# Weight sums of a Strassen product: DVE additions or accumulating transfers from DRAM

## The chip, the cores and the metric

One NeuronCore of one Trainium2 chip runs the whole kernel. The metric is device time in microseconds (us) of one execution, the median of 3 runs. One more execution was taken with the profiler, and all rows below come from that one.

## The reference, cut to what matters

The reference is one encoder block for 512 tokens of width 2048: an RMS norm, one input projection, two attention mixers with gates, the output projection, a residual and a last RMS norm. What matters here is its end:

```python
mixed = jnp.concatenate([out_a, out_b], axis=-1)      # 512 x 2048
x = x + jnp.einsum('bsc,cd->bsd', mixed, w_out)       # w_out 2048 x 2048
return rms_norm(x, final_norm_w)
```

All is float32. The kernel multiplies in a faster format: it splits each operand into a high part (rounded) and a low part (what is left), and a product of two operands takes three matmuls (high x high, low x high, high x low; function `three`, lines 1396 to 1402).

## The kernel before, in words

The kernel is written engine by engine, each with its own instruction stream and semaphores; the order of the work is written out by hand. The output projection comes last. Output columns 0 to 1023 are computed directly. Columns 1024 to 2047 (blocks 2 and 3 of 512 columns) are computed by Strassen's scheme of seven products M1 to M7, over two halves of the tokens, of the input and of the columns. It is done in 16 visits. In each visit one 1 MB piece of `w_out` is used: four slots of 128 x 512, in the buffer `t_raw[v % 4]`.

- Visits 0 to 7 compute M2, M3 and M4. Visits 8 to 15 compute M5, M1, M6 and M7. A late visit has 24 matmuls of 512 columns: 12 for M5 and M1 (slots 0 and 1, group 0), then 12 for M6 and M7 (slots 2 and 3, group 1). Visits 14 and 15 are interleaved (lines 1820 to 1839), with all of both visits' M1 and M5 of the first token quarter ahead of any M6.
- In a late visit the piece holds, in slots 0 to 3, the blocks B11, B22, B12 and B21 of the weights. M1 needs B11 + B22, M5 needs B22, M6 needs B11 + B12, and M7 needs B21 + B22.
- SyncE (SP) loads piece v (line 324) when PE is through with visit v - 4, because there are four buffers. `t_landed[v % 4]` tells of the landing.
- VectorE (DVE) makes the sums in `part_sums(v)` (lines 1248 to 1257): for v of 8 or more, line 1255 adds slots 0 and 1 to slots 2 and 3 (the sums of M6 and M7, 1024 elements a partition), and line 1257 adds slot 1 to slot 0 (the sum of M1, 512 elements).
- ScalarE (ACT) makes the high parts in `part_high(v, g)` (lines 715 to 732), group 0 and then group 1 of each visit, when the sum is there and the `t_hi` buffer of two visits before is free.
- DVE makes the low parts in `part_low(v, g)` (lines 1259 to 1264), in place. PE waits for `t_low[0]` before group 0 and for `t_low[1]` before group 1 (lines 1797 and 1808).
- The order of DVE (lines 1324 to 1344) is: low(v,0), sums(v+1), low(v,1) for v up to 8; then eight additions from PSUM into the rows `y` (lines 1330 to 1336, function `add`, line 1277), which free the banks into which visit 8 accumulates M1, M6 and M7 (`y_added`, lines 1804 to 1817); then low(9,0), low(9,1), sums(10); and then low(v,0), sums(v+1), low(v,1) again.
- GpSimd (POOL) has little to do at this stage: it multiplies finished blocks of `y` by the final gain (`gained`, lines 399 to 402, called at lines 411 to 421), and at the end it scales some of them (line 427).
- The tail behind the last visit is additions from PSUM on DVE, squares on ACT, the root, the scaling and the stores (lines 1365 to 1391, 802 to 815 and 325 to 330).

```python
            for v in range(2, 9):
                part_low(v, 0)
                part_sums(v + 1)
                part_low(v, 1)
...
            for v in range(10, VISITS):
                part_low(v, 0)
                if v < VISITS - 1:
                    part_sums(v + 1)
                part_low(v, 1)
```

Of the kernel before, what the change touches and what calls it, by code (L numbers as in the profile page):

```python
# [6 lines left out]
ALU = mybir.AluOpType  # L7
# [93 lines left out]
def build(nc, w_stream, w_pairs, x_t, x_nat, gains, final_w, tables, out):  # L101
    with ExitStack() as ctx:  # L102
        def sem(name):
            return ctx.enter_context(nc.semaphore(name))
# [8 lines left out]
        def at(name, shape, dt, offset):  # L113
            return nc.alloc_sbuf_tensor_at(name, shape, dt, offset=offset)
# [29 lines left out]
        t_raw = [at(f"t_raw{n}", [P, 4, PART], F32, o) for n, o in enumerate(t_at)]  # L144
# [82 lines left out]
        u_at = [(r_rstd, r_rstd + 3 * KB), (r_rstd + 6 * KB, r_rstd + 9 * KB), (r_kr, r_kr + 3 * KB)]  # L227
        u_at += [(r_mixed + 6 * KB * n, r_mixed + 6 * KB * n + 3 * KB) for n in range(4)] + [(r_mixed + 24 * KB, r_kr + 6 * KB)]
        u_hi = [at(f"u_hi{j}", [P, 3, 256], F32R, o) for j, (o, _) in enumerate(u_at)]
        u_lo = [at(f"u_lo{j}", [P, 3, 256], F32R, o) for j, (_, o) in enumerate(u_at)]  # L230
        fw = [at(f"fw{n}", [P, SEQ], F32, o) for n, o in enumerate((r_ckv + 6 * KB, r_mixed + 28 * KB, r_mixed + 30 * KB, r4 + 32 * KB))]

# [12 lines left out]
        def part_slots(v, g):  # L245
            return slice(2, 4) if g == 1 else slice(1, 2) if v < 8 else slice(0, 2)
# [17 lines left out]
        fold_landed, kr_folded = sem("fold_landed"), sem("kr_folded")  # L264
        y0_landed, y1_landed, y_landed, fw_landed, fws_landed = sem("y0_landed"), sem("y1_landed"), sem("y_landed"), sem("fw_landed"), sem("fws_landed")
        fw1_landed = sem("fw1_landed")
        t_landed = [sem(f"t_landed{n}") for n in range(4)]
        u_summed, u_high, u_low, p_summed, p_high, p_low = sem("u_summed"), sem("u_high"), sem("u_low"), sem("p_summed"), sem("p_high"), sem("p_low")
        t_summed, t_high, t_used, m_done, y_added = sem("t_summed"), sem("t_high"), sem("t_used"), sem("m_done"), sem("y_added")
        t_low = [sem("t_low0"), sem("t_low1")]  # L270
# [63 lines left out]
        def _(pool):  # L334
            def low_part(c, s):
                pool.wait_ge(w_hi_ready, c + 1)
                pool.tensor_tensor(w_lo[:, s % HL, :], w_raw[:, s % RAW, :], w_hi[:, s % HL, :].bitcast(F32), ALU.subtract)\  # L337
                    .then_inc(w_lo_ready, 1)
# [60 lines left out]
            def gained(t, n):  # L399

                cols = slice(SEQ * n, SEQ * n + SEQ)
                pool.tensor_tensor(y[:, t, cols], y[:, t, cols], fw[n][:, :], ALU.mult).then_inc(o_gained, 1)  # L402

            for c in range(WO0 + 4 + AHEAD, WO0 + 16):
                low_part(c, c)
                if c == WO0 + 12:
                    pool.wait_ge(fw_landed, 16)
                    for t in range(TOK):
                        pool.wait_ge(o_squared, t + 2)
                        gained(t, 0)  # L410
            pool.wait_ge(fw1_landed, 16)
            for t in range(TOK):
                pool.wait_ge(o_squared, 4 + t + 2)
                pool.wait_ge(t_low[1], 4 + t)
                gained(t, 1)
            pool.wait_ge(fws_landed, 32)
            for q in range(2):
                pool.wait_ge(o_squared, 8 + q + 2)
                gained(2 * q + 1, 2)
            pool.wait_ge(o_squared, 12)  # L420
            gained(0, 3)

# [13 lines left out]
        def _(act):  # L436
# [218 lines left out]
            for p in range(PAIRS):  # L655
                f = 0
# [58 lines left out]
            def part_high(v, g):  # L715

                if g == 0 and v < 8:
                    act.wait_ge(t_landed[v % 4], 16 * (v // 4) + 16)
                else:
                    act.wait_ge(t_summed, v + 1 if v < 8 else 2 * v - 6 - (g == 1))  # L720
                if v == 0:
                    act.wait_ge(w_used, WO0 + 14)
                elif v == 1:
                    act.wait_ge(o_done, 8)
                elif v < 9:
                    act.wait_ge(t_used, 2 * v - 3 + g)
                elif v == 9:
                    act.wait_ge(m_done, 6 if g else 2)
                else:
                    act.wait_ge(t_used, 2 * v - 5 + g)  # L730
                s = part_slots(v, g)
                act.activation(t_hi[v % 2][:, s, :], t_raw[v % 4][:, s, :], ACT.Copy).then_inc(t_high, 1)  # L732
# [24 lines left out]
            pair_high(4)  # L757
            unit_high(5)
            part_high(0, 0)
            pair_high(5)  # L760
            unit_high(6)
            part_high(0, 1)
            pair_high(6)
            unit_high(7)
            act.wait_ge(u_low, 8)
            residual_rows(0)
            part_high(1, 0)
            pair_high(7)
            part_high(1, 1)
# [49 lines left out]
        def _(dve):  # L819
# [348 lines left out]
            for p in range(PAIRS):  # L1168
                f, late, behind = 0, None, ()
# [78 lines left out]
            def part_sums(v):  # L1248

                raw = t_raw[v % 4]  # L1250
                dve.wait_ge(t_landed[v % 4], 16 * (v // 4) + 16)
                if v < 8:
                    dve.tensor_tensor(raw[:, 2:4, :], raw[:, 0:2, :], raw[:, 2:4, :], ALU.subtract).then_inc(t_summed, 1)
                else:
                    dve.tensor_tensor(raw[:, 2:4, :], raw[:, 2:4, :], raw[:, 0:2, :], ALU.add).then_inc(t_summed, 1)
                    dve.wait_ge(t_summed, 2 * v - 7)
                    dve.tensor_tensor(raw[:, 0, :], raw[:, 0, :], raw[:, 1, :], ALU.add).then_inc(t_summed, 1)  # L1257

            def part_low(v, g):
# [39 lines left out]
            pair_sums(3)  # L1299
            pair_low(3)  # L1300
            part_sums(0)
            pair_sums(4)
            unit_sums(5)
# [6 lines left out]
            unit_low(6)  # L1310
            part_low(0, 1)
            part_sums(1)
            pair_sums(6)
            unit_sums(7)
# [5 lines left out]
            part_low(1, 0)  # L1320
            pair_low(7)
            part_sums(2)
            part_low(1, 1)
            for v in range(2, 9):
# [601 lines left out]
```

## Time and profile before

| what | value |
|---|---|
| median of 3 runs | 672.02 us (671.67 to 672.49) |
| profiled execution, its own time | 671.85 us |
| span of its instructions | 670.1 us |
| PE matmul busy | 654.7 us (98%) |
| DVE busy | 442.2 us (66%) |
| ACT busy | 331.3 us (49%) |
| POOL busy | 280.1 us (42%) |
| HBM read, written | 77.22 MB, 4.19 MB |

The execution's own time is 1.75 us more than the span, which is what lies around the instructions. A matmul row is 0.39 us long but the next one starts 0.227 us after it, so the matmul rows overlap, and the pace is to be read from the starts. The granted clock of TensorE is 1.00 of full speed in the stretches of 10 us from 500 to 660 us.

### The profile page before, as it was taken

Reading aid. Unit: us, or ns where it says so; the run is one execution under the profiler, and the core shown is the slowest. Engines: PE = TensorE matmul, PEld = TensorE weight load, DVE = VectorE, ACT = ScalarE, POOL = GpSimd, SP = SyncE. Lnnn points to the kernel's source line nnn. Section 1 sums busy time; section 2 is a strip of 40 time slices with the busy share of each in tenths; the row PEclk is TensorE's granted clock in tenths of the full one; section 3 lists DMA queues with packets and bytes.
Section 4 is the critical chain, followed back from the end, with each engine's and each line's share of the span. In section 5 each row is a group of like instructions: output and inputs, shape, how many; then the busy total and the mean of one; then the engine's idle time right before and its main releaser. Section 6 shows DMA issues by size and latency. Waiting matters only on the chain. (4 is left out here: it accounts for less than half of the span.)

```text
span 670.1 us, 8800 instructions
## 1 busy us (share of the span) xinstructions
PE 654.7 (98%) x3126; PEld 548.4 (82%) x3126; DVE 442.2 (66%) x702; ACT 331.3 (49%) x623; POOL 280.1 (42%) x135
## 2 busy tenths in 40 slices
PE   9999999999999999999999999999999999999893
PEld 8888888888888888888888888888888888787782
DVE  6788132889684554654645667777553769899985
ACT  6743231311343753763664566877864533543534
POOL 0044443454244433433532526747868483020204
PEclk9999999999999999999999999999999999999997
DMA  8742322232232222222212413213124813576416
GB/s 293 256 141 96 103 94 95 83 105 95 94 94 96 75 83 95 92 65 95 95 64 94 126 35 124 64 64 96 32 72 177 299 65 113 233 259 236 180 64 251
DMA packets 21656, 81.96 MB, mean 122 GB/s; under 512 B 2416, under 2 KB 2672, under 8 KB 19568
## 3 DMA queue, kind: packets, MB, share of 16 engines
q1 hardware_dynamic: 18000, 73.41, 32.1%
q10 hardware_dynamic: 3616, 8.02, 3.4%
q8 instruction: 25, 0.41, 0.2%
q14 instruction: 15, 0.12, 0.1%
HBM read 77.22 MB, written 4.19 MB: 122 GB/s over the span
## 5 line engine op out<-in xcount | busy, mean ns | idle before, releaser
L337 POOL TENSOR_TENSOR w_lo<-w_raw,w_hi 128x1024 fp32r<-128x1024 f32 x84 | 206.0, 2458 | 269.7 <-ACT w_hi L442 269.6
L1398 PE MATMUL bank<-x_hi,w_hi 128*128 128x512 f32 x496 | 193.7, 390 | 0.0
L1401 PE MATMUL bank<-x_hi,w_lo 128*128 128x512 f32 x496 | 193.3, 390 | 0.0
L1402 PE MATMUL bank<-x_lo,w_hi 128*128 128x512 f32 x496 | 193.2, 390 | 0.0
L442 ACT ACTIVATE w_hi<-w_raw 128x1024 fp32r<-128x1024 f32 x93 | 98.1, 1055 | 130.0 <-PE bank L1398 109.1
L1402 PEld LDWEIGHTS bank<-x_lo,w_hi 128*128 128x128 f32 x496 | 93.1, 188 | 19.7
L1398 PEld LDWEIGHTS bank<-x_hi,w_hi 128*128 128x128 f32 x496 | 93.2, 188 | 18.8 <-DVE mixed L1078 0.5
L1401 PEld LDWEIGHTS bank<-x_hi,w_lo 128*128 128x128 f32 x496 | 93.2, 188 | 18.0
L402 POOL TENSOR_TENSOR y<-y,fw 128x512 f32<-128x512 f32 x11 | 17.6, 1616 | 80.1 <-ACT junk L705 44.4
L1398 PE MATMUL bank<-w_hi,mx_hi 128*128 128x512 f32 x128 | 50.3, 393 | 0.0
L1402 PE MATMUL bank<-w_lo,mx_hi 128*128 128x512 f32 x128 | 49.9, 390 | 0.0
L1401 PE MATMUL bank<-w_hi,mx_lo 128*128 128x512 f32 x128 | 49.9, 390 | 0.0
L732 ACT ACTIVATE t_hi<-t_raw 128x1024 fp32r<-128x1024 f32 (+1 forms) x32 | 29.8, 950 | 37.7 <-DVE t_raw L1257 19.5
L540 ACT ACTIVATE bank<-pa,st_a 128x128 f32<-128x128 f32 x64 | 22.8, 356 | 43.2 <-DVE st_a L992 43.2
L1264 DVE TENSOR_TENSOR t_lo<-t_raw,t_hi 128x1024 fp32r<-128x1024 f32 (+1 forms) x32 | 35.2, 1120 | 5.3 <-ACT t_hi L732 5.3
L1007 DVE TENSOR_TENSOR pta_lo<-bank,pta_hi 128x512 fp32r<-128x512 f32 x16 | 11.1, 692 | 32.1 <-ACT pta_hi L547 32.0
L1402 PEld LDWEIGHTS bank<-w_lo,mx_hi 128*128 128x128 f32 x128 | 24.0, 188 | 5.1
L1401 PEld LDWEIGHTS bank<-w_hi,mx_lo 128*128 128x128 f32 x128 | 24.1, 188 | 4.7
L895 DVE TENSOR_TENSOR t<-bank,sin_r 32x512 f32<-32x512 f32 x40 | 27.5, 687 | 0.5
L1398 PEld LDWEIGHTS bank<-w_hi,mx_hi 128*128 128x128 f32 x128 | 24.0, 188 | 4.6
L1015 DVE TENSOR_TENSOR mixed<-bank,o_low 64x256 f32<-64x256 f32 x32 | 13.5, 422 | 21.6 <-ACT o_low L554 21.4
L1398 PE MATMUL bank<-t_hi,mx_hi 128*128 128x512 f32 x64 | 25.3, 395 | 2.3 <-DVE t_lo L1264 2.2
(242 smaller groups left out, 1236.0 us busy)
## 6 DMA issues: line engine op xcount, KB each, us to landing
w_raw<-w_stream SPq DMA_DIRECT2D x93, 512.0 KB, 3.3
t_raw<-w_pairs SPq DMA_DIRECT2D x15, 1024.0 KB, 4.7
y<-x_nat ACTq DMA_DIRECT2D x4, 1024.0 KB, 5.3
out<-y SPq DMA_DIRECT2D x8, 512.0 KB, 3.0
xs<-x_t SPq DMA_DIRECT2D x4, 512.0 KB, 5.5
mixed<-x_t SPq DMA_DIRECT2D x4, 512.0 KB, 5.6
t_raw<-w_pairs ACTq DMA_DIRECT2D x1, 1024.0 KB, 7.7
fw<-final_w ACTq DMA_DIRECT2D x4, 256.0 KB, 5.6
```

The costliest lines, as they stand in the source:

```text
L337: pool.tensor_tensor(w_lo[:, s % HL, :], w_raw[:, s % RAW, :], w_hi[:, s % HL, :].bitcast(F32), ALU.subtract)\
L402: pool.tensor_tensor(y[:, t, cols], y[:, t, cols], fw[n][:, :], ALU.mult).then_inc(o_gained, 1)
L442: act.activation(w_hi[:, s % HL, :], w_raw[:, s % RAW, :], ACT.Copy).then_inc(w_hi_ready, 1)
L540: act.activation(B[4][:, P * k:P * k + P], pa[:, slot, k, :], ACT.Exp, bias=st[:, 1, k:k + 1], scale=A_SCALE, accum_out=st[:, 3, k:k + 1])
L732: act.activation(t_hi[v % 2][:, s, :], t_raw[v % 4][:, s, :], ACT.Copy).then_inc(t_high, 1)
L895: ins = dve.tensor_tensor(t2[32 * q:32 * q + 32, :], src[32 * o:32 * o + 32, :], sin[32 * q:32 * q + 32, :], ALU.mult)
L1007: dve.tensor_tensor(pta_lo[:, :], B[6][:, :], pta_hi[:, :].bitcast(F32), ALU.subtract).then_inc(a_pt_lo, 1)
L1015: ins = dve.tensor_tensor(out_e, by_head[h, e], o_low[h, :, :, :], ALU.add)
L1264: dve.tensor_tensor(t_lo[v % 4][:, s, :], t_raw[v % 4][:, s, :], t_hi[v % 2][:, s, :].bitcast(F32), ALU.subtract).then_inc(t_low[g], 1)
L1398: ins = pe.matmul(dst, ah, bh, start=start, stop=False, skip_group_check=goes_on)
L1401: pe.matmul(dst, al, bh, start=False, stop=False, skip_group_check=goes_on)
L1402: return pe.matmul(dst, ah, bl, start=False, stop=stop, skip_group_check=goes_on)
```

## The change: what it does

POOL gets a new step, `piece_added(v)`: it waits until piece v has landed and issues a transfer that reads slots 0 and 1 of that piece from DRAM again (512 KB) and adds them to slots 2 and 3 in the buffer. A new semaphore `t_added[v % 4]` tells when it has landed. The eight steps are placed between the `gained` steps of POOL. Line 1255 of DVE and the wait behind it are gone, and ACT's high part of group 1 waits for `t_added` in place of `t_summed`. Eight DVE instructions of 1024 elements go, eight transfers of 512 KB come, and the rest of the order of each engine stays.

```diff
+            def piece_added(v):
+                pool.wait_ge(t_landed[v % 4], 16 * (v // 4) + 16)
+                pool.dma_start(t_raw[v % 4][:, 2:4, :], w_pairs[v, :, 0:2, :], accum_op=ALU.add).then_inc(t_added[v % 4], 16)
+
             pool.wait_ge(fw1_landed, 16)
             for t in range(TOK):
                 pool.wait_ge(o_squared, 4 + t + 2)
                 pool.wait_ge(t_low[1], 4 + t)
                 gained(t, 1)
+                if t == 2:
+                    piece_added(8)
+            piece_added(9)
+            piece_added(10)
+            piece_added(11)
+            piece_added(12)
             pool.wait_ge(fws_landed, 32)
             for q in range(2):
                 pool.wait_ge(o_squared, 8 + q + 2)
                 gained(2 * q + 1, 2)
+                piece_added(13 + q)
+            piece_added(15)
             pool.wait_ge(o_squared, 12)
             gained(0, 3)
...
                 if g == 0 and v < 8:
                     act.wait_ge(t_landed[v % 4], 16 * (v // 4) + 16)
+                elif g == 1 and v >= 8:
+                    act.wait_ge(t_added[v % 4], 16 * (v // 4) - 16)
                 else:
-                    act.wait_ge(t_summed, v + 1 if v < 8 else 2 * v - 6 - (g == 1))
+                    act.wait_ge(t_summed, v + 1)
...
                 if v < 8:
                     dve.tensor_tensor(raw[:, 2:4, :], raw[:, 0:2, :], raw[:, 2:4, :], ALU.subtract).then_inc(t_summed, 1)
                 else:
-                    dve.tensor_tensor(raw[:, 2:4, :], raw[:, 2:4, :], raw[:, 0:2, :], ALU.add).then_inc(t_summed, 1)
-                    dve.wait_ge(t_summed, 2 * v - 7)
                     dve.tensor_tensor(raw[:, 0, :], raw[:, 0, :], raw[:, 1, :], ALU.add).then_inc(t_summed, 1)
```

## Rows read from the trace of the kernel before

**Rows 1.** The page: span, and busy time of each engine.

```profile
span 670.1 us, 8800 instructions
PE 654.7 (98%) x3126; PEld 548.4 (82%) x3126; DVE 442.2 (66%) x702; ACT 331.3 (49%) x623; POOL 280.1 (42%) x135
```

**Rows 2.** Who waited for whom, 580 to 670 us: total, times, longest.

```profile
PEld bank L1398 <- DVE t_lo L1264: 4.0, 5, 2.4
PEld bank L1398 <- DVE y L1277: 1.2, 2, 0.7
```

**Rows 3.** Timeline of PE: start, duration; in brackets the idle time before.

```profile
611.31 0.39 PE L1398 MATMUL bank<-t_hi,u_hi 128*128 128x512 f32 x1
...
617.68 0.50 PE L1398 MATMUL bank<-t_hi,u_hi 128*128 128x512 f32 x1
...
628.09 0.50 PE L1398 MATMUL bank<-t_hi,mx_hi 128*128 128x512 f32 x1 [1.95 <-DVE t_lo L1264]
...
657.97 0.39 PE L1402 MATMUL bank<-t_lo,mx_hi 128*128 128x512 f32 x1
```

**Rows 4.** Timeline of DVE, 604 to 630 us.

```profile
604.00 1.64 DVE L1255 TENSOR_TENSOR t_raw<-t_raw 128x1024 f32<-128x1024 f32 x1 [0.59 <-DMA t_raw<-w_pairs]
605.67 0.69 DVE L1257 TENSOR_TENSOR t_raw<-t_raw 128x512 f32<-128x512 f32 x1
...
608.63 1.22 DVE L1255 TENSOR_TENSOR t_raw<-t_raw 128x1024 f32<-128x1024 f32 x1
...
610.50 1.22 DVE L1264 TENSOR_TENSOR t_lo<-t_raw,t_hi 128x1024 fp32r<-128x1024 f32 x1
611.63 4.87 DVE L1277 TENSOR_TENSOR y<-y,bank 128x512 f32<-128x512 f32 x8
...
618.68 1.22 DVE L1255 TENSOR_TENSOR t_raw<-t_raw 128x1024 f32<-128x1024 f32 x1
...
624.15 1.67 DVE L1257 TENSOR_TENSOR t_raw<-t_raw 128x512 f32<-128x512 f32 x1
625.74 3.43 DVE L1264 TENSOR_TENSOR t_lo<-t_raw,t_hi 128x1024 fp32r<-128x1024 f32 x2
```

**Rows 5.** Timeline of POOL in the same stretch.

```profile
602.95 1.61 POOL L402 TENSOR_TENSOR y<-y,fw 128x512 f32<-128x512 f32 x1 [2.36 <-DVE t_lo L1264]
623.42 3.53 POOL L402 TENSOR_TENSOR y<-y,fw 128x512 f32<-128x512 f32 x2 [18.87 <-ACT junk L705]
```

**Rows 6.** Instructions on the buffers `t_raw`: durations min/median/max ns, first and last start.

```profile
L1255 DVE TENSOR_TENSOR t_raw<-t_raw x8: 1211/1218/1637, 604.0 to 641.7; 128x1024 f32<-128x1024 f32 x8
```

**Rows 7.** Timeline of the loads that SP issues (pieces 8, 9 and 15).

```profile
599.26 0.33 SPq L324 DMA_DIRECT2D t_raw<-w_pairs  x1
...
603.34 0.33 SPq L324 DMA_DIRECT2D t_raw<-w_pairs  x1
...
636.58 0.33 SPq L324 DMA_DIRECT2D t_raw<-w_pairs  x1
```

**Rows 8.** The page: DMA issues, KB each, median us from issue to landing.

```profile
t_raw<-w_pairs SPq DMA_DIRECT2D x15, 1024.0 KB, 4.7
...
out<-y SPq DMA_DIRECT2D x8, 512.0 KB, 3.0
...
t_raw<-w_pairs ACTq DMA_DIRECT2D x1, 1024.0 KB, 7.7
```

**Rows 9.** Timeline of ACT: the high parts (10,0) and (10,1), and (15,1).

```profile
620.66 2.01 ACT L732 ACTIVATE t_hi<-t_raw 128x1024 fp32r<-128x1024 f32 x2 [8.03 <-DVE t_raw L1257]
...
647.52 1.06 ACT L732 ACTIVATE t_hi<-t_raw 128x1024 fp32r<-128x1024 f32 x1 [1.66 <-PE bank L1402]
```

**Rows 10.** Stretches: us, busy PE, PEld, DVE, ACT, POOL, PEclk, DMA share, GB/s.

```profile
603.30:607.42 4.12, 4.12 (x20) 3.42 (x19) 3.49 (x4) 2.09 (x2) 1.25 (x1) 1.00 0.67 259
607.42:611.50 4.08, 4.08 (x19) 3.38 (x19) 4.05 (x5) 1.99 (x3) 0.00 (x0) 1.00 0.69 255
628.00:650.00 22.00, 21.91 (x97) 18.05 (x97) 19.30 (x20) 8.38 (x8) 0.00 (x0) 1.00 0.28 96
```

More of the change, by code:

```diff
@@ L266, in build @@
         fw1_landed = sem("fw1_landed")
-        t_landed = [sem(f"t_landed{n}") for n in range(4)]
+        t_landed, t_added = ([sem(f"{name}{n}") for n in range(4)] for name in ("t_landed", "t_added"))
         u_summed, u_high, u_low, p_summed, p_high, p_low = sem("u_summed"), sem("u_high"), sem("u_low"), sem("p_summed"), sem("p_high"), sem("p_low")
```

## The prediction, written before the changed kernel was run

> **What bounds the kernel now.** I read the page first. PE is busy for 654.7 of 670.1 us and DVE for 442.2 [rows 1], so DVE work saved is worth something only where PE waits for DVE. The view of waits of the last 90 us gives those places: the weight loads wait five times for a low part, 4.0 us in all and 2.4 at most, and twice for the additions into `y`, 1.2 us [rows 2]. The timeline of PE gives their size. Visit 8 starts at 611.31 and visit 9 at 617.68 [rows 3]; 24 matmuls at the pace of 0.227 us are 5.45 us, so 0.92 us are lost there. From 617.68, a visit and a half is 8.17 us, which ends at 625.9, but group 1 of visit 10 starts at 628.09: 2.2 us lost. The last matmul starts at 657.97. Without any loss it would start at 611.31 + 191 x 0.227 = 654.7. So 3.3 us is all that the visits from 8 on can give back. All the rest of the span is PE work or comes before the change.
>
> The timeline of DVE says why PE waits. Visit 8 needs the banks that the eight additions free; they start at 611.63, behind low(8,1) at 610.50, behind the sums of piece 9 at 608.63 [rows 4]. Visit 10 needs low(10,1), which ends at about 628.0. It comes behind line 1255 and line 1257 of piece 11, and POOL's two `gained` at 623.42 [rows 5] stretch it: line 1257 takes 1.67 us in place of 0.69, and the two lows at 625.74 take 3.43 in place of 2.44 [rows 4].
>
> **The sum, part by part.** *Removed:* eight instructions of line 1255, 1218 ns median [rows 6], 9.8 us of DVE time. From 628 to 650 us PE is busy for 21.91 of 22.00 us [rows 10], so five of the eight are worth nothing in themselves. The three that count are those of pieces 8, 9 and 10/11.
>
> *Visit 10.* The additions end about 616.4, and the two lows of visit 9 at 618.68 [rows 4]. Then only 0.69 for line 1257; ACT's high part 1.0 (two in 2.01, [rows 9]); low(10,0) 1.22: 621.7. Line 1257 of piece 11, 0.69, and low(10,1), 1.22: 623.6. PE wants it at 625.9. The 2.2 us are gone, with 2.3 us to spare. That is the gain, if the rest stays where it is.
>
> *Added:* on each visit the wait of ACT for the new transfer. Call X the time from POOL's issue to the landing. What matters is where this wait is on the path. There are two places.
>
> First, piece 8. Its load is issued at 599.26 [rows 7] and DVE sees it at 604.00 [rows 4]. So POOL issues the add at 604.0, behind the third `gained`, which is over by then; it lands at 604.0 + X. ACT's high part takes 1.06 [rows 9], and low(8,1) 1.22, paced 1.13 by the two rows of [rows 4] at 610.50 and 611.63, and 0.1 for two semaphores. The eight additions are queued on DVE behind low(8,1), and visit 8 of PE and low(9,0) wait for them. They start at 606.3 + X, against 611.63 now. So X = 5.3 keeps them in place, and each us more costs one. Less can give at most the 0.92 + 0.2 us of visits 8 and 9, down to X = 4.2; then the load of piece 9 (issued at 603.34, [rows 7], so 608.1) is late next.
>
> Second, piece 15. Its load is issued when PE is through with visit 11: at 636.58 now [rows 7], 634.4 with the 2.2 us gone. It lands 4.7 later [rows 8], 639.1, and the add at 639.1 + X. ACT can begin high(15,1) when PE is through with visit 13, now 647.52 [rows 9], then 645.3. So X up to 6.2 is covered, and from 6.3 on each us costs another one, because low(15,1) and M6 of visit 14 stand right behind. Pieces 9 to 14 have more room: piece 10 lands at about 612.2, its add at 612.2 + X, and low(10,1) can start at 622.4, so X could be 8 or 9 there.
>
> Gain = 2.2 - (X - 5.3) up to X = 6.3, and 2.2 - (X - 5.3) - (X - 6.3) beyond. It is 2.0 at 5.5, 0 at 6.9, -2.2 at 8, -4.2 at 9.
>
> *Price of X.* No row shows a transfer that POOL issues or one that adds. The low end is a plain transfer of 512 KB, 3.0 us. The high end is three passes of that size one after the other (read the source, read the destination, write), 9 us; the worst row of a 1 MB transfer is 7.7 [rows 8]. Between them, the 1 MB load at 4.7 [rows 8] is the nearest, since an add reads as many bytes as it does: 512 KB from DRAM and 512 KB of the destination. To this I add 0.8 for the issue and for company: loads 9 and 10 are under way while add 8 runs, the DMA engines being busy for 0.67 and 0.69 of these stretches [rows 10]. X = 5.5; both ends stay in the range.
>
> By the Trainium skill (DMA: Bandwidth & Descriptors, Anatomy of one DMA) a transfer that POOL issues takes about 2.0 us and its bytes over 436 GB/s. That is an estimate of 3.2 us for 512 KB, and the full 3.3 us of gain; the page gives no rate for one that accumulates, and no run here shows either.
>
> *POOL's queue.* Eight waits for landings now stand in it. Behind the first is `gained(3,1)`, which moves from 602.95 [rows 5] to after 604; it will hold DVE up to 1 us there, on line 1257 of piece 8 or low(7,1). PE wants low(7,1) at 608.6 and DVE has saved 1.2 us, so it costs nothing. `gained(3,2)` moves behind the issue for piece 13, from about 625.2 to about 627 or 629. DVE then needs only 3 us of work in a visit of 5.45, which covers it, and its reader stands in the tail at 654 or later. The loads of SP are on another queue and keep their times, but share the DMA engines; DVE needs load 9 at 608.6, and it is there at 608.1; if it is late by up to 0.8 at X = 5.5 nothing changes, since DVE would be waiting for low(8,1). The tail moves with PE.
>
> **The rivals.** *Slower: the wait for the add replaces the DVE addition (X over 7.6).* The place is low(8,1), ahead of the eight additions, and then high(15,1). What speaks for it: DVE did the same sum in 1.22 us, any transfer needs 3 us and more, and the sum is queued in front of work that PE waits for. Against it: X must be over 2.9 us longer than a 1 MB load. From X = 7.6 it is over 0.2% slower; at X = 8.5 it gives +3.2, 675.2 us. 0.28.
>
> *Between (X from 6.2 to 7.6).* The gain at visit 10 is given back at visit 8: about 672 at X = 6.9. 0.20. *POOL's issue is held up by DVE* is one way into it. In this stretch DVE runs back to back [rows 4] and one instruction of it is 1.22 us, so an issue held for one of them gives X = 6.7 and a gain of 0.4, some 671.6 us. The time is from the rows alone. The Trainium skill (SBUF — State Buffer, Who interferes with whom) has a rule behind this: the writing of POOL's descriptors is locked out by some DVE instructions. It exempts the tensor-tensor kind, the only kind that DVE has here, and marks the reason as inferred; no run here shows it yet. I give it 0.05 of the 0.20.
>
> *The full 3.3 us (X up to 4.2):* 668.7 us, 0.12. *It does not do what it says,* for one because the transfers crowd the loads out and every load comes late: the load share of 0.67 against 512 KB more for each 1 MB would show it first at 603 to 612. It is in the 0.28.
>
> **How the numbers follow.** The profiled execution took 671.85 us, 0.17 below the median of 672.02. X = 5.5 gives 671.85 - 2.0 = 669.85, and as a median 670.0. The cases: X up to 6.2, 0.52 (of it 0.12 for the full gain); 6.2 to 7.6, 0.20; above, 0.28. A measurement can tell about 0.2%, 1.34 us, from no change: gain over 1.34 is X under 6.2, loss over 1.34 is X over 7.6. So 0.52, 0.20 and 0.28. The range goes from the full gain, 668.6, to X = 8.8, which is +3.8, 675.8; above it is 0.12 to 0.15, below it 0.05. The forecast's own range is 668.6 to 670.7.
>
> **What would show it.** Right: DVE has 694 instructions; PE shows no idle time before group 1 of visit 10; the row of eight additions starts at about 611.8; landings of the adds take 5 to 6 us; high(15,1) still ends its wait on PE. Wrong: the additions start after 613, PE waits for `y` by 2 us and more in visit 8, or PE waits for low(15,1) at the end. If X is under 4.5, the loss at visit 8 is gone as well.

## The result, and the profile after

The changed kernel takes 677.28 us (median of 4 runs, 677.07 to 677.45) against 672.25 us before: ratio 1.0074, 95% interval 1.0061 to 1.0087. The forecast was 670.0 us, so it is slower by 5.0 us where 2.0 less was expected, and outside the range. The profiled execution took 677.33 us with a span of 675.5.

The page of the changed kernel, against [rows 1] and [rows 8]. In the part on DMA queues the columns are packets, MB, and share of the 16 engines' time over the span; in the part on issues, count, KB each and median us to landing.

```profile
span 675.5 us, 8800 instructions
PE 656.2 (97%) x3126; PEld 548.7 (81%) x3126; DVE 433.2 (64%) x694; ACT 330.8 (49%) x623; POOL 285.7 (42%) x143
...
q1 hardware_dynamic: 18000, 73.41, 31.2%
q0 software_dynamic: 1152, 4.19, 3.4%
...
HBM read 81.42 MB, written 4.19 MB: 127 GB/s over the span
...
t_raw<-w_pairs SPq DMA_DIRECT2D x15, 1024.0 KB, 5.6
...
t_raw<-w_pairs POOLq DMA_DIRECT2D x8, 512.0 KB, 7.7
```

DVE has its eight instructions less and 9 us less work, as the diff says. The new transfers land 7.7 us after their issue, and the loads have become slower with them. Queue q0, the one of the adding transfers, moves 4.19 MB in 3.4% of the engines' time, q1 73.41 MB in 31.2%. That is 5.5 us a MB against 2.9: a byte that is added costs nearly twice a byte that is copied.

The waits of the last part, 580 to 676 us, against [rows 2].

```profile
ACT t_hi L746 <- DMA t_raw<-w_pairs: 28.0, 8, 6.3
DVE t_lo L1276 <- ACT t_hi L746: 16.7, 9, 3.2
...
PEld bank L1410 <- DVE t_lo L1276: 6.0, 6, 1.6
...
PEld bank L1410 <- DVE y L1289: 3.2, 2, 2.9
```

ACT waits eight times for the new transfer, DVE for ACT, and PE for DVE: the longest wait of PE is now that for the additions into `y`, 2.9 us, where it was 0.7.

The timelines of DVE, of POOL and of PE, against [rows 4], [rows 5] and [rows 3].

```profile
612.59 1.23 DVE L1276 TENSOR_TENSOR t_lo<-t_raw,t_hi 128x1024 fp32r<-128x1024 f32 x1 [3.22 <-ACT t_hi L746]
613.73 4.86 DVE L1289 TENSOR_TENSOR y<-y,bank 128x512 f32<-128x512 f32 x8
...
653.65 1.23 DVE L1276 TENSOR_TENSOR t_lo<-t_raw,t_hi 128x1024 fp32r<-128x1024 f32 x1 [2.31 <-ACT t_hi L746]
```

```profile
604.05 1.03 POOL L413 DMA_DIRECT2D t_raw<-w_pairs  x1 [3.74 <-DMA t_raw<-w_pairs]
...
608.95 0.88 POOL L413 DMA_DIRECT2D t_raw<-w_pairs  x1 [2.53 <-DMA t_raw<-w_pairs]
615.45 0.86 POOL L413 DMA_DIRECT2D t_raw<-w_pairs  x1 [5.62 <-DMA t_raw<-w_pairs]
```

```profile
615.06 0.80 PE L1410 MATMUL bank<-t_hi,u_hi 128*128 128x512 f32 x1 [2.48 <-DVE y L1289]
...
663.00 0.39 PE L1414 MATMUL bank<-t_lo,mx_hi 128*128 128x512 f32 x1
```

POOL issues the add of piece 8 at 604.05, and it lands 7.4 us later. The additions start at 613.73, which is what the prediction's formula gives for X = 7.4 (606.3 + 7.4). The add of piece 10 is issued only at 615.45, because its load took 8.0 us in place of 4.8. The eight adds took 7.4, 9.6, 7.5, 9.7, 7.9, 10.2, 5.9 and 6.8 us in the order of the pieces.

The stretches of the changed kernel (columns as in [rows 10]):

```profile
603.30:607.42 4.12, 4.12 (x19) 3.40 (x19) 3.66 (x2) 1.98 (x2) 2.37 (x2) 1.00 0.82 262
607.42:611.50 4.08, 4.08 (x19) 3.38 (x18) 1.92 (x3) 0.01 (x1) 0.88 (x1) 1.00 1.00 223
...
616.00:618.00 2.00, 2.00 (x6) 1.46 (x5) 2.00 (x5) 0.00 (x0) 0.31 (x1) 0.50 1.04 387
618.00:640.00 22.00, 22.00 (x96) 17.85 (x95) 15.56 (x13) 10.98 (x14) 5.22 (x5) 0.99 0.98 259
```

The DMA engines are busy all the time from 607 to 646, at 0.98 to 1.04 by this count, where [rows 10] has 0.69 from 607 to 611; and in that stretch they move 223 GB/s where they moved 255. From 615.0 to 618.4 the granted clock of TensorE is 0.50, the lower of its two levels, right after PE had stood still for 2.5 us.

**A ledger of PE.** A late visit needs 24 matmuls at 0.227 us. What a stretch takes above that, read from the starts of the matmul rows, is lost there. A wait at the start of a visit is counted with the visit before it. All kernels of this study stand in it, so that each experiment below can be read from its line (us, of one profiled execution each; medians and intervals are given with each):

| kernel | visit 8 | 9 and 10 | 11 to 13 | 14 and 15 | sum |
|---|---|---|---|---|---|
| before | 0.9 | 2.4 | 0.0 | 0.1 | 3.3 |
| after | 4.4 | 0.0 | 1.3 | 3.0 | 8.6 |
| pool_plain | 2.1 | 0.1 | 0.0 | 0.0 | 2.3 |
| sp_plain | 0.9 | 0.2 | 0.0 | 0.0 | 1.1 |
| pool_half | 2.3 | 0.1 | 0.0 | 0.0 | 2.4 |
| reorder | 1.7 | 1.9 | 0.4 | 0.0 | 4.0 |
| late_gain | 0.9 | 0.3 | 0.1 | 0.7 | 2.0 |
| dve_all_but_11 | 1.0 | 0.2 | 0.0 | 0.0 | 1.2 |
| dve_8 | 0.0 | 1.1 | 1.2 | 4.6 | 6.9 |
| dve_all_but_8 | 2.7 | 3.8 | 0.1 | 0.1 | 6.7 |
| pool_9_11 | 0.0 | 0.6 | 0.0 | 0.1 | 0.6 |
| dve_8_12_to_15 | 0.0 | 0.8 | 1.5 | 0.6 | 2.9 |
| dve_all_but_15 | 0.9 | 2.4 | 0.0 | 0.2 | 3.5 |

From before to after: visits 9 and 10 give back their 2.4 us, as forecast; visit 8 takes 3.4 more, visits 11 to 15 take 4.2 more. That is +5.3 of the span's +5.4. One execution can be off by almost 1 us in visit 8: reorder changes nothing ahead of visit 10 and has 1.7 there, because POOL's multiplication at 603.58 ran beside DVE's long sum at 603.96 and made it 2.31 us long, against 1.64 in the kernel before.

### The profile page after: what moved, and what is told of

Same layout as the page of the kernel before. It is cut to its first block and busy times, and to the rows that moved or that the text cites. A ratio compares the mean times of both kernels' runs of the same rounds, so it can differ in the third digit from the quotient of the medians.

```text
span 675.5 us, 8800 instructions
## 1 busy us (share of the span) xinstructions
PE 656.2 (97%) x3126; PEld 548.7 (81%) x3126; DVE 433.2 (64%) x694; ACT 330.8 (49%) x623; POOL 285.7 (42%) x143
## 3 DMA queue, kind: packets, MB, share of 16 engines
q1 hardware_dynamic: 18000, 73.41, 31.2%
q0 software_dynamic: 1152, 4.19, 3.4%
HBM read 81.42 MB, written 4.19 MB: 127 GB/s over the span
## 5 line engine op out<-in xcount | busy, mean ns | idle before, releaser
L1276 DVE TENSOR_TENSOR t_lo<-t_raw,t_hi 128x1024 fp32r<-128x1024 f32 (+1 forms) x32 | 37.2, 1189 | 16.7 <-ACT t_hi L746 16.7
L1413 PEld LDWEIGHTS bank<-w_hi,mx_lo 128*128 128x128 f32 x128 | 24.1, 188 | 4.6
```

The source lines that it names most:

```text
L1276: dve.tensor_tensor(t_lo[v % 4][:, s, :], t_raw[v % 4][:, s, :], t_hi[v % 2][:, s, :].bitcast(F32), ALU.subtract).then_inc(t_low[g], 1)
L1413: pe.matmul(dst, al, bh, start=False, stop=False, skip_group_check=goes_on)
```

## The experiments

Three theories of the long landing were put up: it is the adding that is dear (A), it is POOL's way of issuing (B), or it is the 512 KB more for each 1 MB (C).

**The same transfers without adding (pool_plain).** Slots 2 and 3 are overwritten, so this kernel computes something else; only its times count. The same holds for sp_plain and, in part, for pool_half.

```diff
-                pool.dma_start(t_raw[v % 4][:, 2:4, :], w_pairs[v, :, 0:2, :], accum_op=ALU.add).then_inc(t_added[v % 4], 16)
+                pool.dma_start(t_raw[v % 4][:, 2:4, :], w_pairs[v, :, 0:2, :]).then_inc(t_added[v % 4], 16)
```

> The changed kernel, with the eight transfers of POOL made plain: they overwrite slots 2 and 3 with slots 0 and 1 and add nothing, so M6 and M7 lack a part of their weights. Theory A (it is the adding that is slow: it costs the DMA engines twice as much a byte): issue to landing falls from 7.4 to 10.2 us to some 4 to 5, the loads go back from 8.0 to about 5.3, PE does not wait in visit 8 for over 1 us, and the time is 669 to 670.5 us. Theory B (it is POOL's way of issuing that is slow): landing stays at 7 us or more and the time at 676 to 677.5. Theory C (512 KB more for every 1 MB is too much, whoever moves it): landing 6 us or more, loads 7 us or more, time 673 to 677.

Measured: 670.31 us, ratio 0.9971 (0.9958 to 0.9983) to the kernel before. The queues from 603 to 653 us, first of the changed kernel, then of this one (MB, share of the engines in this stretch):

```profile
q0 software_dynamic: 1152, 4.19, 46.2%
q1 hardware_dynamic: 1029, 7.38, 41.4%
```

```profile
q0 software_dynamic: 1152, 4.19, 24.1%
...
t_raw<-w_pairs SPq DMA_DIRECT2D x7, 1024.0 KB, 6.6
t_raw<-w_pairs POOLq DMA_DIRECT2D x8, 512.0 KB, 5.5
```

46.2% of 50 us over 4.19 MB is 5.5 us of engine time a MB with the adding; 24.1% is 2.9 without it, and the loads take 2.8. Taking away the adding alone, with the same bytes, the same queue and the same waits, gives 7.0 us. That is theory A. Not all went as it said: the landing is 5.5 and not 4 to 5, the loads take 6.6 and not 5.3, and visit 8 still loses 2.1 where it was to wait no more than 1.

**The same plain transfers, issued by SP (sp_plain).**

```diff
+            def second_half(v):
+                sp.wait_ge(t_landed[v % 4], 16 * (v // 4) + 16)
+                sp.dma_start(t_raw[v % 4][:, 2:4, :], w_pairs[v, :, 0:2, :]).then_inc(t_added[v % 4], 16)
+
             for v in range(4, VISITS):
...
                 sp.dma_start(t_raw[v % 4][:, :, :], w_pairs[v, :, :, :]).then_inc(t_landed[v % 4], 16)
+                if v >= 9:
+                    second_half(v - 1)
+            second_half(15)
...
             def piece_added(v):
+                return
```

> The same plain transfers, issued by SP in place of POOL, each behind the load of the next piece. Again nothing is added. Theory A: like the plain transfers of POOL within 1 us, landing 3.3 to 4.5 us. Theory B: landing 3.3 to 4.5 us here and 7 us or more from POOL. Theory C: as slow as POOL's, landing 6 us or more.

Measured: 669.29 us, ratio 0.9952 (0.9936 to 0.9968). The landing is 5.5 us at the median, longer than expected, and the loads 5.4. For piece 8 it is 5.4 against 6.3 from POOL; low(8,1) is then in time for the additions to start at 611.30, as before the change. This kernel is 8.0 us faster than the changed one, and pool_plain 7.0. So theory B has at most 1 us of the 8, and not even that is shown to be POOL's, since SP's transfers also stand in one queue with the loads, in another order. Theory C is out: with all the traffic of the changed kernel (81.42 MB read), visits 11 to 15 lose nothing. This is also the test of the gain: with a sum that is free, visits 9 and 10 give back 2.2 us.

**Adding half as much (pool_half).**

```diff
-                pool.dma_start(t_raw[v % 4][:, 2:4, :], w_pairs[v, :, 0:2, :], accum_op=ALU.add)
+                pool.dma_start(t_raw[v % 4][:, 2, :], w_pairs[v, :, 0, :], accum_op=ALU.add)
```

> The changed kernel with accumulating transfers of half the size: only slot 0 is added to slot 2 (256 KB each), and the sum for M7 is left out. If the price is one per byte, landing falls from a median of 7.7 to about 4.5 to 5.5 us, the loads from 8.0 to about 6, the share of the DMA engines' time that POOL's queue takes halves, and the time is 669.5 to 671.5 us. If it is a fixed price of an issue or a wait, landing stays at 6.5 us or more and the time above 674.

Measured: 671.09 us (one run). The queue line from 603 to 653 us of this kernel:

```profile
q0 software_dynamic: 1152, 2.10, 25.1%
```

2.10 MB that are added take as much of the engines as 4.19 MB that are copied (24.1%): the price goes nearly by the byte and is double. The landing fell only to 5.8 at the median and the loads only to 7.0, both more than forecast, but the late losses are gone. In visit 8 the additions start at 612.66, 1.07 us sooner than in the changed kernel, and PE loses 2.3 there in place of 4.4: 2.1 us for 1.07. The other 1.0 is the clock, which stays at 1.00 here: from 616.08 to 617.79 the matmuls of the changed kernel start 0.43 us apart in place of 0.227.

**The gain without any transfer (reorder, late_gain).** Of the gap before group 1 of visit 10 the prediction named two causes, DVE's order and POOL's two multiplications.

```diff
                 part_low(v, 0)
+                if v == 10:
+                    part_low(v, 1)
                 if v < VISITS - 1:
                     part_sums(v + 1)
-                part_low(v, 1)
+                if v > 10:
+                    part_low(v, 1)
```

> The kernel before, without any transfer of POOL: on DVE low(10,1) goes ahead of the sums of piece 11, and nothing else is changed. If the 2.2 us that PE lost before group 1 of visit 10 came from the place of those sums in DVE's order, the gap is gone and at most 1 us of it comes back before visit 11, for which low(11,0) is now later: 670.0 to 671.3 us. If POOL's multiplications or ACT's squares there were the cause, the gap stays and the time is 672.

```diff
             for q in range(2):
                 pool.wait_ge(o_squared, 8 + q + 2)
+                pool.wait_ge(t_low[1], 11 + 2 * q)
                 gained(2 * q + 1, 2)
```

> The kernel before, with its DVE additions and without any transfer of POOL; POOL's two multiplications that ran at 623.42 wait for low(10,1) and low(12,1). If they took the same SBUF time from DVE at the worst place, line 1257 of piece 11 goes back from 1.67 to 0.69 us and low(10,1) from about 2.3 to 1.2, the gap of 2.3 us of PE before group 1 of visit 10 falls to 0.1 to 0.4, and the time is 669.8 to 670.6 us. If DVE's own order is the cause, the gap stays over 1 us and the time at 671 or more.

Measured: reorder 671.63 us, ratio 0.9987 (0.9976 to 0.9998), between what its two expectations said; late_gain 670.75 us, ratio 0.9976 (0.9967 to 0.9985). With the new order the gap before group 1 of visit 10 is gone, and 1.7 us of it come back at the start of visit 11, where at most 1 was expected. The timeline of DVE in the kernel reorder shows why:

```profile
624.67 2.32 DVE L1255 TENSOR_TENSOR t_raw<-t_raw 128x1024 f32<-128x1024 f32 x1
627.02 1.66 DVE L1257 TENSOR_TENSOR t_raw<-t_raw 128x512 f32<-128x512 f32 x1
```

The sums of piece 11 now run beside POOL's multiplications (624.06 to 628.13) and take 3.98 us in place of the 1.9 of 1.22 and 0.69 [rows 4], and low(11,0) waits for them. In late_gain these multiplications come later, and DVE's order and additions are as they were. From the matmul before the gap of visit 10 to the one behind it were 2.33 us before the change; here they are 0.28, close to the pace of 0.227:

```profile
626.08 0.39 PE L1403 MATMUL bank<-t_lo,u_hi 128*128 128x512 f32 x1
626.36 0.50 PE L1399 MATMUL bank<-t_hi,mx_hi 128*128 128x512 f32 x1
```

So POOL's work beside DVE is needed for the gap. It is not enough by itself: dve_all_but_11 below leaves the multiplications where they are and takes DVE's long sum of piece 11 away, and the gap is gone too. Each of the two fills what room the other leaves. late_gain has a new loss of 0.5 us ahead of low(15,0), in visit 14. Its trace shows the moved multiplication of 636.21 beside DVE's long sum of piece 14 at 637.20, which takes 2.30 us in place of 1.22, and no idle time on DVE from there to the low parts of visit 14.

**Which pieces may be added by a transfer.** In the next six kernels a list `ON_DVE` says which pieces DVE adds as before; POOL skips them.

```diff
             def piece_added(v):
+                if v in ON_DVE:
+                    return
...
                 else:
+                    if v in ON_DVE:
+                        dve.tensor_tensor(raw[:, 2:4, :], raw[:, 2:4, :], raw[:, 0:2, :], ALU.add).then_inc(t_summed, 1)
+                        dve.wait_ge(t_summed, sums_before(v) + 1)
                     dve.tensor_tensor(raw[:, 0, :], raw[:, 0, :], raw[:, 1, :], ALU.add).then_inc(t_summed, 1)
```

Piece 15 alone, by itself (`ON_DVE` = 8 to 14):

> Only piece 15 is added by POOL's transfer, when no other transfer is under way. Landing is the price of an accumulating transfer of 512 KB by itself: by the share of the DMA engines' time (5.5 us a MB, 2.9 us for this one) plus some 2.5 us of issue and completion, 5 to 6 us, against 4.0 us for the plain one of POOL and 3.6 for that of SP at the same place. If the adding is limited by something other than crowding, it is 6.8 us or more as in the changed kernel. Up to 6.2 us it is covered, and the time is that of before, 672 us.

Measured: 672.12 us (one run), as before. From 641 to 648 us, with no other data transfer under way:

```profile
q0 software_dynamic: 144, 0.52, 48.9%
...
t_raw<-w_pairs POOLq DMA_DIRECT2D x1, 512.0 KB, 6.0
```

6.0 us is the price of one such add with nothing beside it. 48.9% of 7 us is 3.4 us of all 16 engines, against 2.9 for each of the eight in the changed kernel. The plain transfer at the same place took 4.0 us from POOL (pool_plain) and 3.6 from SP (sp_plain).

Piece 8 alone (`ON_DVE` = 9 to 15), and all but piece 8 (`ON_DVE` = 8):

> Only piece 8 is added by POOL's transfer, DVE adds the others. Landing 6 to 7 us beside load 9. DVE is then busy with the sums of piece 9 at 608.6 and comes to low(8,1) when ACT is through. With a landing of 6.5 the additions start at 612.8 and PE loses 1.2 us more in visit 8 than before: 672.8 to 674 us; with over 7.2 the clock falls as well and it is 674.5 or more.

> The changed kernel, but piece 8 is added on DVE; POOL adds 9 to 15. By the ledger the 4.4 us that PE loses in visit 8, the half clock included, go back to about 1.2 or a little less, the clock stays at full, and the late losses of visits 12 to 15 (4.6 us) stay, because they come from loads and adds that crowd each other: 673.5 to 674.5 us. If the late losses are only a shift handed on from visit 8, they shrink with it: 671 or less.

Measured: dve_all_but_8 675.59 us, ratio 1.0047 (1.0028 to 1.0066); dve_8 674.78 us, ratio 1.0027 (1.0008 to 1.0046). Both are slower than expected, dve_8 by 0.3 us. In dve_all_but_8 the landing is 6.8 and PE stands still for 1.9 us in visit 8; the gap of visit 10 is there as before. What the expectation lacked is the clock, which was to fall only with a landing over 7.2. PE's rows behind the two waits, and the stretches around visit 10:

```profile
615.10 0.50 PE L1426 MATMUL bank<-t_hi,u_hi 128*128 128x512 f32 x1 [1.88 <-DVE y L1305]
...
630.23 0.50 PE L1426 MATMUL bank<-t_hi,mx_hi 128*128 128x512 f32 x1 [1.95 <-DVE t_lo L1292]
```

```profile
628.00:631.00 3.00, 1.05 (x5) 0.67 (x4) 3.00 (x2) 1.99 (x2) 1.09 (x1) 1.00 0.58 243
631.00:634.00 3.00, 3.00 (x9) 2.32 (x8) 2.96 (x4) 0.80 (x1) 0.00 (x0) 0.57 0.00 0
```

The same wait of 1.95 us in the kernel before [rows 3] left the clock at 1.00 [rows 10]; here one of 1.88 us stands ahead of it, at 613 to 615, and the clock falls to 0.57 at the mean of the 3 us from 631 on. In dve_8 the losses of visit 8 are gone, 0.0 us, better than the 1.2 expected. DVE's timeline in dve_8:

```profile
610.08 4.86 DVE L1305 TENSOR_TENSOR y<-y,bank 128x512 f32<-128x512 f32 x8
```

The additions start 1.6 us sooner than in [rows 4], because piece 9's long sum, 1.2 us, is off DVE, and all of this execution runs 0.3 earlier. But the losses behind it stay and grow: 1.1 us at the start of visit 11, 1.2 in it, and 4.6 in visits 14 and 15. The add of piece 14 took 10.4 us beside load 15, PE then stood still for 2.7 us, and the clock fell again, to 0.60 at the mean of 649 to 653 us:

```profile
649.49 0.55 PE L1426 MATMUL bank<-t_hi,u_hi 128*128 128x512 f32 x1 [2.70 <-DVE t_lo L1292]
```

```profile
649.00:653.00 4.00, 3.52 (x9) 2.82 (x10) 2.72 (x4) 1.06 (x1) 0.00 (x0) 0.60 0.00 0
```

Piece 11 alone (`ON_DVE` = 8, 9, 10, 12 to 15), and pieces 9 and 11:

> One accumulating transfer only, that of piece 11; DVE adds the other seven. If the three places of the ledger are what decides (the adds of 8 ahead of the additions, those of 12 to 15 that crowd loads and come late, and the one place that gains, visit 10), this keeps the gain alone: landing 5 to 6 us beside little other traffic, no PE gap before group 1 of visit 10, 669.6 to 670.4 us. If an accumulating transfer hurts wherever it runs, by the traffic or by POOL's work, it stays at 671.5 or more.

> POOL's transfers add pieces 9 and 11 only, DVE the other six. With piece 9 off DVE the additions into y start 1.2 to 1.6 us sooner (610.1 where DVE added piece 8 alone, against 611.65), and with piece 11 off DVE the gap before group 1 of visit 10 is gone. If the traffic of two such transfers keeps its distance from the loads that matter, PE loses under 0.6 us from visit 8 on and the time is 668.6 to 669.4 us. If load 11 or 12 is late from it, a wait of 0.5 to 2 us comes in visits 10 to 12 and the time is 670 to 671.5.

Measured: dve_all_but_11 670.31 us, ratio 0.9972 (0.9961 to 0.9982); pool_9_11 669.55 us, ratio 0.9968 (0.9955 to 0.9982). One transfer in the right place gives the whole gain of visit 10, although it takes 9.2 us to land, where 5 to 6 was expected, and slows load 12 to 8.4. In this kernel POOL's multiplications run at 623.46 for 3.55 us, as in [rows 5]:

```profile
623.46 3.55 POOL L411 TENSOR_TENSOR y<-y,fw 128x512 f32<-128x512 f32 x2 [5.08 <-ACT junk L728]
```

With piece 9 as well, the loss of visit 8 goes too in the profile; of 3.3 us, 0.6 are left. The two intervals overlap, so the times don't show that piece 9 adds anything. Both are faster than both kernels of this case.

Pieces 9, 10 and 11 (`ON_DVE` = 8, 12 to 15):

> POOL adds pieces 9, 10 and 11; DVE adds 8 and 12 to 15. If the late losses of 5.6 us of the kernel with only piece 8 on DVE come from the adds of 12 to 15 and what they do to loads, they are gone, and the time is 668.7 to 670 us; some wait may be left in visits 10 to 12, where load 12 goes beside add 11. If they come from POOL's transfers in general, 672 or more.

Measured: 673.53 us, ratio 1.0019 (0.9999 to 1.0038), so not told apart from the kernel before. The first expectation is missed by over 3 us. The number of the second, 672 or more, holds, but its reason fits the profile in part only: the losses of visits 11 to 15 are 2.1 us, against 5.8 in dve_8. The runs go from 671.4 to 676.2 us and the profiled one took 671.6, so the profile shows less than the median has. DMA issues from 603 to 653 us:

```profile
t_raw<-w_pairs POOLq DMA_DIRECT2D x3, 512.0 KB, 9.2
fw<-final_w ACTq DMA_DIRECT2D x2, 256.0 KB, 11.2
```

Three adds in a row are enough to fill the engines: the third lands after 10.0 us, the final gain (256 KB twice) after 11.2 at the median, and POOL's multiplications, which wait for it, begin at 629.48 in place of 623.42. There they run beside low(11,1), and the two low parts at 629.90 take 4.55 us in place of 2.44; visit 11 loses 1.5. The 0.8 us at its start come earlier: add 10 lands at 621.88, and ACT, which makes high(10,1) only then and has its squares behind it, comes to high(11,0) at 625.82. What makes the other executions slower still is open.

## Why the prediction was wrong

Both signs that it named for being wrong came: the additions started after 613 (613.73), and PE waited for `y` by over 2 us in visit 8 (2.9). Step by step:

- *What can be gained, and where (3.3 us; 0.9 in visit 8 and 2.2 at visit 10)*: right. pool_9_11 got 2.7 us of it in the profile, sp_plain 2.2.
- *The gap of visit 10 goes*: right, in every kernel that takes piece 11 off DVE. Its cause was stated in two parts, DVE's long sum and POOL's multiplications, and both are needed: without either one (dve_all_but_11, late_gain) it is gone.
- *The wait moves to low(8,1), the additions start at 606.3 + X*: right to 0.1 us (613.73 at X = 7.4).
- *The price of X = 5.5*: the first step that failed. It took the adding transfer for a copy of 1 MB, 4.7 us, and 0.8 for the issue and for company. Alone it is 6.0 us, and in the changed kernel 5.9 to 10.2; at the two places that the sum counts it is 7.4 (piece 8) and 6.8 (piece 15). A byte that is added costs the DMA engines 5.5 us a MB, a copied one 2.8 or 2.9.
- *"The loads of SP are on another queue and keep their times"*: the second step that failed, and the heavier one. With X = 7.4 and 6.8 the prediction's own formula gives 2.2 - 2.1 - 0.5 = -0.4 us, a time of about 672.4. The other 5 us are not in X. About 1 is the clock in visit 8; some 3.7 are the losses of visits 11 to 15 beyond the 0.5 of piece 15, and they come where loads and adds hold each other up; 0.3 in visit 8 are left over. One load takes 2.9 us of all 16 engines and one add as much, together 5.8, and a late visit lasts 5.45: the eight adds need 23 us in 50, the loads 21, and loads took up to 9.7 us, adds up to 10.2. The prediction had half of this in hand: it took an add for a copy of 1 MB when it priced X, and for 512 KB, half a sentence among the rivals, when it priced the loads. Counted in bytes it is harmless, as sp_plain shows; what counts is engine time. Its check, the share of the DMA engines from 603 to 612, went from 0.67 and 0.69 to 0.82 and 1.00.
- *"Pieces 9 to 14 have more room", "X could be 8 or 9"*: right for 9 to 11 in the changed kernel, wrong for 12 to 14, where the load comes late as well. In dve_8 and dve_8_12_to_15 visit 11 loses too.
- *The second place, piece 15, covered up to X = 6.2*: right in its form. At 6.0 (dve_all_but_15) it costs 0.1 us. In the changed kernel visits 14 and 15 lose 3.0, in two parts. The prediction had only the second, 1.4 us for low(15,1). The first is 1.3 us for low(15,0), which stands on DVE behind low(14,1), and so behind the add of piece 14 that landed at 647.87.
- *Each us of X costs one*: too little where PE stood still for 2.5 us. 1.07 us more of delay cost 2.1 in visit 8 (pool_half against after), with the clock at 0.50 from 615.0 to 618.4. In pool_plain, with X = 6.3 and the clock at 1.00, it holds: 1.2 us more are lost in visit 8 than before, where the formula gives 1.0.
- *The rival that came nearest in time* was the first one, X over 7.6, with 675.2 us for X = 8.5. At the places that it names X was 7.4 and 6.8, which is the case between, of about 672 us. What carried the time to 677.3 was the last rival, the transfers that crowd the loads; it had no price of its own.
- *POOL's issue held up by DVE*: not seen. The eight issues take 856 to 1031 ns each, and each has a tensor-tensor instruction of DVE beside it. What the Trainium skill (SBUF — State Buffer, Who interferes with whom) exempts, the tensor-tensor kind, is not in the way here either.
- By the Trainium skill (DMA: Bandwidth & Descriptors, Anatomy of one DMA) a transfer of 512 KB from POOL was estimated at 3.2 us; the plain one of pool_plain took 4.0 at the quietest place. The measurement decides, and the accumulating one is 2 us above that.

## What to carry to other kernels

An accumulating transfer does not make a sum free: it moves 1.2 us of DVE work to 3 us of all DMA engines, and every load that runs beside it pays too. Before putting a transfer in the place of an instruction, add up the engine time of all transfers of that stretch, not their bytes, and ask what is queued behind the instruction that will wait for it. And use it only where an engine is late: of the eight sums here one was worth moving (2.0 us), a second did no harm beside it, and with the other six the kernel is 8 us slower. Look first for what else makes the engine late: moving two multiplications of POOL got 1.5 us without any transfer. The two cures together were not tried.

## What was not expected of the hardware

- Accumulating transfers took 5.5 us of the DMA engines' time a MB and plain ones 2.8 to 2.9. At half the size it was 6.0 (2.10 MB in 25.1% of 50 us), and for one add alone 6.5 (0.52 MB in 48.9% of 7 us).
- A POOL multiplication of 128x512 with two SBUF operands holds up DVE's sum beside it by about 1 us, for each one (1.67 in place of 0.69, 2.32 in place of 1.22). Moving two of them was worth 1.5 us of the kernel's time, against 2.0 for taking DVE's long sum of piece 11 away.
- The granted clock fell to its lower level after PE had stood still for 2.5 us (after, 0.50 from 615.0 to 618.4) or 2.7 us (dve_8), and after two stops of 1.88 and 1.95 us (dve_all_but_8, 0.57 for 631 to 634 us), but not after a single one of 1.95 us in the kernel before.
